# Fused hybrid blocks in f32r: the split weight tiles begin 64 bytes further on in SBUF

## What is computed

```python
# first block
h = layer_norm(ALPHA * h + 0.5 * swiglu(h, w_gate, w_up, w_down))        # width 2816
h = layer_norm(ALPHA * h + token_mixers(h))    # HGRN2 recurrence and spatial gating
h = layer_norm(ALPHA * h + cross_attention(h, mem))                      # 256 memory tokens
h = layer_norm(ALPHA * h + 0.5 * swiglu(h, w_gate2, w_up2, w_down2))
# second block
z = (rms_norm(h) * (1 + scale) + shift) @ w_in
y = [neighbourhood_attention(z), short_conv(z), conformer_conv(z)]       # three branches
h = h + gate * ((ga * (y[0] @ oa) + gb * (y[1] @ ob) + gc * (y[2] @ oc)) @ w_o)
```

## The kernel before

| tiles | begin at, before | mod 256 |
|---|---|---|
| raw | 16512 | 128 |
| w_hi, w_lo | 32896, 49280 | 128 |
| a_hi, a_lo | 82048, 98432 | 128 |
| hid_hi, hid_lo | 135808, 180864 | 128 |
| side_hi, side_lo | 144000, 152192 | 128 |
| mix_h, mix_l, y_hi, y_lo, m_hi, m_lo, xpt, memv | | 128 |
| ctx_hi, ctx_lo | 205632, 213824 | 64 |
| consts, mean_d, mean_w, mean_p | 115904 and on | 192 |
| npr, npt, ck_c, cv_c | 215840 and on | 32 |

## Time and profile before

### The profile page before, as it was taken

The page is one execution under the profiler, slowest core; times in us unless marked ns, Lnnn a source line. Parts: engine busy times, 40 slices in busy tenths (PEclk is TensorE's granted clock), DMA queues, the critical chain, the costliest instruction groups (busy, mean ns, idle before and its releaser), DMA issues.

```text
span 1706.6 us, 22901 instructions
## 1 busy us (share of the span) xinstructions
PE 1691.5 (99%) x8500; PEld 1394.7 (82%) x8500; DVE 994.7 (58%) x1341; ACT 683.6 (40%) x975; POOL 166.8 (10%) x158
## 2 busy tenths in 40 slices
PE   9999999999999999999999999999999999999999
PEld 7888888888787888888888888877778787788887
DVE  5333339987965784666333333457976869844442
ACT  4222232246454465434222223346454445732330
POOL 0000000112004521013000000013011020000000
DMA  5333247633122353223332233323333222243331
GB/s 216 98 98 98 91 138 231 222 121 119 52 98 66 109 182 137 67 82 123 98 98 94 92 130 117 109 87 118 85 99 95 86 83 86 74 123 109 104 109 62
DMA packets 51476, 188.05 MB, mean 110 GB/s; under 512 B 5776, under 2 KB 6288, under 8 KB 50512
## 3 DMA queue, kind: packets, MB, share of 16 engines
q1 hardware_dynamic: 44640, 161.50, 29.7%
q10 hardware_dynamic: 5184, 16.00, 2.9%
q0 software_dynamic: 1584, 9.60, 1.6%
HBM read 182.89 MB, written 4.19 MB: 110 GB/s over the span
## 4 chain that ended last, share of the span: by engine, by line
PE 89%; DVE 7%; ACT 2%; issue 1%; DMA 0%; POOL 0%; SPq 0%; DVEq 0%; ACTq 0%; POOLq 0%
PE proj L422 83%; DVE w_lo L414 1%; PE aux L1859 1%; PE aux L1846 1%; PE aux L1619 1%; PE aux L1836 1%; DVE y L2016 0%; ACT w_hi L407 0%; DVE score L1221 0%; DVE qk L1264 0%; DVE md L1242 0%; PE aux L566 0%; DVE qk L1265 0%; PE aux L1839 0%; DVE md L1241 0%
## 5 line engine op out<-in xcount | busy, mean ns | idle before, releaser
L414 DVE TENSOR_TENSOR w_lo<-raw,w_hi 128x1024 fp32r<-128x1024 f32 x300 | 380.5, 1270 | 388.8 <-ACT w_hi L407 382.0
L422 PE MATMUL proj<-a_hi,w_hi 128*128 128x512 f32 (+1 forms) x1536 | 600.8, 391 | 3.3 <-DVE a_lo L909 1.8
L422 PE MATMUL proj<-a_hi,w_lo 128*128 128x512 f32 (+1 forms) x1536 | 591.3, 385 | 0.0
L422 PE MATMUL proj<-a_lo,w_hi 128*128 128x512 f32 (+1 forms) x1536 | 591.0, 385 | 0.0
L407 ACT ACTIVATE w_hi<-raw 128x1024 fp32r<-128x1024 f32 x300 | 315.3, 1053 | 233.4 <-PE proj L422 164.3
L422 PEld LDWEIGHTS proj<-a_hi,w_hi 128*128 128x128 f32 x1536 | 288.5, 188 | 67.9 <-issue 5.8
L422 PEld LDWEIGHTS proj<-a_lo,w_hi 128*128 128x128 f32 x1536 | 288.7, 188 | 58.4 <-issue 2.9
L422 PEld LDWEIGHTS proj<-a_hi,w_lo 128*128 128x128 f32 x1536 | 288.5, 188 | 58.5
L422 PE MATMUL proj<-hid_hi,w_hi 128*128 128x512 f32 (+1 forms) x374 | 142.6, 381 | 0.0
L422 PE MATMUL proj<-hid_hi,w_lo 128*128 128x512 f32 (+1 forms) x374 | 140.9, 377 | 0.0
L422 PE MATMUL proj<-hid_lo,w_hi 128*128 128x512 f32 (+1 forms) x374 | 140.8, 377 | 0.0
(11 more groups left out here) (368 smaller groups left out, 2011.1 us busy)
## 6 DMA issues: line engine op xcount, KB each, us to landing
raw<-stream SPq DMA_DIRECT2D x303, 512.0 KB, 3.5
ctxk<-ada_in ACTq DMA_DIRECT2D x12, 512.0 KB, 3.7
ctxv<-ada_in ACTq DMA_DIRECT2D x12, 512.0 KB, 3.9
out<-h ACTq DMA_DIRECT2D x7, 256.0 KB, 2.0
h<-x_in SPq DMA_DIRECT2D x3, 512.0 KB, 8.7
btab<-rpb_in POOLq DMA_DIRECT2D x4, 384.0 KB, 3.5
cond_row<-cond_in ACTq DMA_DIRECT2D x1, 1024.0 KB, 5.9
side<-mem_in POOLq DMA_DIRECT2D x1, 1024.0 KB, 5.2
```

The source lines that it names most:

```text
L414: nc.vector.tensor_tensor(w_lo[:, st.slot], raw[:, st.slot], w_hi[:, st.slot].bitcast(F32), ALU.subtract).then_inc(lo_ready, 1)
L422: mm = nc.tensor.matmul(dst, a, b, start=start and n == 0, stop=stop and n == 2)
```

## The change

Two tiles of 64 bytes that nothing uses are declared, one ahead of `w_hi` and one behind `w_lo`. No instruction is added, removed or moved on any engine; only addresses differ, and line numbers grow by 2.

```diff
         raw = sb("raw", [P, RING, SB * P])
+        sb("shift_before", [P, 16])
         w_hi = sb("w_hi", [P, RING, SB * P], F32R)
         w_lo = sb("w_lo", [P, RING, SB * P], F32R)
+        sb("shift_behind", [P, 16])
         h = sb("h", [P, KD, T])
```

## The result

The changed kernel takes 1721.03 us (median of 4 runs, 1719.3 to 1727.21) against 1708.08 us: ratio 1.0081, 95% interval 1.0062 to 1.0100. It is slower by 0.8%, where 2.5% faster was forecast.

A forecast was written before the change was run, and what follows sets the result against it. PE was taken as the bound, through its matmul rate. 46.6 us gross less 4.6 us off the path left 42.0; span 1706.6 became 1664.6, plus 1.6 gave 1666.2 us, range 1636 to 1712.

The forecast's parts named there:

- the price of the 6618 matmuls that go to offset 192: Matmuls of L422 leaving offset 0 for 192: each taken to gain 6.7 ns, the value read from `ctx`.
- a fixed sum per matmul, not a share of its columns: PE start distances: the extra over streaming, 13.4 ns at 512 columns and 13.3 at 256, read as fixed per matmul.
- from offset 64 to 192 by symmetry: L422 matmuls: 192 is as far from 0 as the 64 of `ctx`, on the other side, so the same 6.7 ns.
- -42.0 in all: Span on PE: 6263 matmuls of L422 outside stretches where other engines set the chain, 6.7 ns off each.
- two streams that hinder each other where their places are equal: PE's reading of both operands: a same remainder hinders, two steps of 6.7 ns at offset 0, one at 64.
- The bound: Whole kernel: PE, busy 99% of the span and 89% of the chain, sets the end by matmul rate.
- The period of 256 bytes: Tile places: offsets between the operands were counted as remainders modulo 256 bytes.
- That remainders set `ctx` apart: `ctx` against `side`, same shape and line: remainder 64 in place of 128 makes it 113.3 ns, not 120.0.
- the other end of a term taken as 0: The 96 `ctx` matmuls going from offset 64 to 0: loss taken as 0, at most 0.6 us.
- The zeros for splits: `split_hi` and `split_lo` with mixed remainders: 1% either way on DVE, hidden behind PE, taken as 0.
- The slower rival: Main stretch at offset 192: distance 233.4 ns, 42 us added, 1750 us; chance 0.15.
- the mirror of 64: Matmuls at 192: stationary operand 64 behind instead of ahead, so one step of 6.7 ns more, not less.

The follow-up runs named there:

- e3: Kernel before plus 192 unused bytes behind `w_lo`, activations moved, offset (stationary less moving remainder, modulo 256) 64: 1743.01 us, ratio 1.0206.
- e10: Matmuls alone, computation left out: 512 columns at offsets 0 to 252 bytes in steps of 4, either or both tiles moved, other column counts; 226.7 ns at offset 0.
- e4: Kernel before plus 256 unused bytes behind `w_lo`, bringing the offset back to 0 modulo 256: 1708.57 us, ratio 1.0004.
- e9: Kernel of matmuls alone, computation left out, offsets 0 to 480 bytes in steps of 32, four column counts: at 512 columns 226.7 ns at 0, 233.3 at 64.
- e5: Kernel before plus 64 unused bytes ahead of `w_hi` only; weights and activations keep offset 0, only `raw` differs from them: 1708.18 us, ratio 0.9998.
- e8: Kernel before with padding between `w_hi` and `w_lo` and behind `w_lo`, so `w_lo` alone goes to offset 64: 1731.47 us, ratio 1.0137.
- e12: Kernel before with `w_hi` and `w_lo` as parts of one tile beginning 4 bytes further on, everything else 256 bytes: offset 4, 1739.84 us, ratio 1.0187.

## Why the prediction was wrong

**The step that failed** is the price of the 6618 matmuls that go to offset 192: "I take the value of `ctx`, 6.7 ns gained". It carried a price over two gaps at once. One is from 256 columns to 512: e3 put the moving activations at the very offset that `ctx` had, and 512 columns take 233.3 ns there, 6.6 more than at 0, while 256 columns gain 2.2 or 6.7 (117.8 or 113.3). Under it lay the sentence that the extra is "a fixed sum per matmul, not a share of its columns", drawn from two column counts that happened to show 13.3 both; 448 columns, also at offset 0, have 206.7 - 448 / 2.4 = 20.0 (e10). The other gap is from offset 64 to 192 by symmetry: 64 and 192 aren't alike at 512 columns (233.3 and 229). Measured, the term is +10.6 us for 6054 matmuls of 512 columns, 1.75 ns each over all distances and 2 ns in the main stretch, -1.0 us for the 563 of 256 columns and +0.9 us for the weights-moving ones, in place of -42.0 in all.

**The picture behind it** failed too: two streams that hinder each other where their places are equal. Offset 0 is no collision but the lowest distance that 64 offsets have at 512 columns.

**What held.** The bound: PE sets the end, and the whole change of the span is a change of distances on it. The period of 256 bytes, shown by e4 and e9. That remainders set `ctx` apart: it went to 120 ns like the rest, and its +0.6 us was the other end of a term taken as 0 (96 x 6.7 ns). The zeros for splits (e5), statistics and transfers. The slower rival had the right sign and the right place to look, a distance above 226.7, but its reason (the mirror of 64) and its 6.7 ns per matmul are not what the changed kernel has; 1750 was too much by 29 us. The weights-moving strips, at the offset of `ctx`, did tell the offsets apart, by being the worse of the two.

**The rules.** The Trainium skill (SBUF — State Buffer, Who interferes with whom) has PE's two read ports independent and PE never waiting. By that rule the time would have stayed at 1708 us, nearer to 1721 than the 1666 forecast; but the place of one f32r operand against the other moves the rate by 3%, from 226.7 to 233.4 ns, in e9 with TensorE alone. Whether its ports are what waits no run shows. The figure of 215.7 ns for a warm matmul (TensorE: Matmul & The Clock Gate, Wait — 56ns, not 53.3ns?) is 2.4 ns above the stream. The f32 passes have the same extra, 429.2 for 426.7 ns, but f32r at 512 columns never came under 226.7.

**What stays open.** What makes the 13.3 ns and its changes in f32r. The runs show that offset and place set the distance, not by what mechanism: why all three distances move when one load of three moves (e8), why there are two steady rates at one offset, and why 4 bytes of either operand matter. Not tried were 16-bit operands, f32r matmuls that follow each other without a weight load for each, and the fine steps with the moving tile beyond 4, 8 and 16 bytes.

No version beats the kernel before: it stands at offset 0, the lowest that was found for 512 columns. For the 256-column strips another offset is worth 1 us (the changed kernel) to 2 us (e3: 72.3 us for the 563 in place of 74.3).

## What to carry to other kernels

A price read from one shape holds for that shape; before it is carried to six thousand matmuls of another, ask which rows have both the new column count and the new offset, and if none has, keep the two signs as likely as each other. For a kernel of f32r matmuls back to back, the remainders modulo 256 of the two operands were worth 2% here. Matmuls alone measure them within a millisecond, and the whole kernel repeated their answer at each of the eight offsets that were tried in both, if the same operand is moved and the column count is the same. And a small tile added anywhere ahead of a weight tile can move a TensorE-bound kernel by that much: if an edit that seems harmless costs 1 to 2%, compare the start-to-start distance first.

## What the runs showed that I had not expected

- f32r, 512 moving columns, 128 stationary: 226.7 ns at offsets 0, 100, 120, 132, 144, 156, 228 and 252, up to about 237 at the others of 64; at multiples of 32 the same again 256 bytes on.
- The same offset of 252 bytes takes 226.7 ns with the stationary operand displaced and 236.7 with the moving one 4 bytes behind a multiple of 32, alone (e10) and in the whole kernel (e12).
- f32r, 256 columns at offset 64: 117.8 or 113.3 ns, both steady, in one run (e3).
- f32 passes: 429.2 ns for 512 columns and 215.8 for 256, at five offsets.
- At 448 columns offset 0 is the worst of four (206.7 against 199.9 at 192), at 384 columns 173.3 at 0, 32 and 192 and up to 176.7 elsewhere, at 128 columns 111.6 everywhere.
- A stationary block of 32 columns at offset 32 takes 240.0 ns, longer than one of 128.
